# Inverse roots in columns of tokens, and six units of products kept back in the last chunk

## The reference

```python
x = x + 0.5 * swiglu_ffn(x, norm_ffn1, w_ffn1_in, w_ffn1_out)     # d_model 1024, d_ff 2816
h = rmsnorm(x, norm_mix) @ w_in                                    # columns for two head groups
y_ssd = rmsnorm(ssd(h) * silu(z), norm_ssd_out)                    # 512 wide
y_nsa = rmsnorm(sparse_attention(h), norm_nsa_out)                 # 512 wide, three branches
x = x + concatenate([y_ssd, y_nsa]) @ w_out
x = x + memory_attention(x, norm_mem_q, w_mem_q, w_mem_out)        # 4 heads, 256 memory rows
x = x + 0.5 * swiglu_ffn(x, norm_ffn2, w_ffn2_in, w_ffn2_out)
y = rmsnorm(x, norm_final)
rmsnorm(x, g) = x * rsqrt(mean(x * x) + 1e-6) * g
swiglu_ffn(x, g, w_in, w_out): gate, up = split(rmsnorm(x, g) @ w_in); return (silu(gate) * up) @ w_out
```

## Time and profile before

| | |
|---|---|
| median of three runs | 2847.9 us (2844.55 to 2849.76) |
| profiled execution | 2840.38 us |
| its span, first to last instruction | 2838.7 us |
| mean granted clock of TensorE | 0.973 of 2.4 GHz |
| TensorE busy (matmul) | 2697.9 us, 95% |
| VectorE busy | 1418.0 us, 50% |
| ScalarE busy | 717.4 us, 25% |
| GpSimd busy | 344.1 us, 12% |
| first feed-forward stage ends | near 817 us |
| output projection and queries | 1778.6 to near 1931 us |
| second feed-forward stage, final norm and stores | 2011 to 2838.7 us |

### The profile page before, as it was taken

One profiled execution on the slowest core, in us unless ns is written; L12 is line 12 of the kernel. 1 busy time (PEld: TensorE's weight loads), 2 busy tenths in 40 slices (PEclk: granted clock), 3 DMA queues, 4 the chain that ended last, 5 costly groups with the idle time before them and its releaser, 6 DMA issues. The chain is left out here.

```text
span 2838.7 us, 43914 instructions
## 1 busy us (share of the span) xinstructions
PE 2697.9 (95%) x17720; PEld 2529.8 (89%) x17720; DVE 1418.0 (50%) x2949; ACT 717.4 (25%) x1466; POOL 344.1 (12%) x294
## 2 busy tenths in 40 slices
PE   8999999999989998989789988899999999999996
PEld 7999999999989997879557765797899999999996
DVE  7444444444466222335567753676644444444445
ACT  5111111111042212212456652435411111111102
POOL 0000000000020000101157761220100000000003
PEclk9999999999999999989889998899999999999998
DMA  6111111111025325114120004102211111111101
GB/s 215 45 45 45 46 45 45 45 45 45 16 96 67 53 76 192 59 38 116 42 61 16 2 22 177 60 23 90 75 45 45 45 45 45 45 45 45 41 5 63
DMA packets 62989, 168.42 MB, mean 59 GB/s; under 512 B 10468, under 2 KB 43780, under 8 KB 52996
## 3 DMA queue, kind: packets, MB, share of 16 engines
q1 hardware_dynamic: 57716, 150.36, 16.8%
q10 hardware_dynamic: 3104, 9.41, 0.9%
q0 software_dynamic: 1968, 5.77, 0.6%
HBM read 145.90 MB, written 23.69 MB: 60 GB/s over the span
## 5 line engine op out<-in xcount | busy, mean ns | idle before, releaser
L523 DVE TENSOR_TENSOR ffn_gated<-ffn_gate_up,ffn_inv_rms 128x728 f32<-128x728 f32 x132 | 120.6, 914 | 536.9 <-PE ffn_gate_up L206 536.7
L204 PE MATMUL ffn_gate_up<-h_ffn_hi,ffn_up_hi 128*128 128x364 f32 (+1 forms) x1056 | 349.1, 331 | 15.1 <-DVE h_ffn_lo L102 11.5
L204 PE MATMUL ffn_down<-ffn_act_hi,ffn_down_hi 128*128 128x364 f32 (+1 forms) x1056 | 349.9, 331 | 7.8 <-issue 6.2
L204 PE MATMUL ffn_gate_up<-h_hi,ffn_up_hi 128*128 128x364 f32 (+1 forms) x1056 | 347.5, 329 | 2.6 <-DVE ffn_gated L523 1.0
L205 PE MATMUL ffn_gate_up<-h_ffn_lo,ffn_up_hi 128*128 128x364 f32 (+1 forms) x1056 | 347.8, 329 | 0.0
L205 PE MATMUL ffn_down<-ffn_act_lo,ffn_down_hi 128*128 128x364 f32 (+1 forms) x1056 | 347.8, 329 | 0.0
L206 PE MATMUL ffn_gate_up<-h_ffn_hi,ffn_up_lo 128*128 128x364 f32 (+1 forms) x1056 | 347.7, 329 | 0.0
L206 PE MATMUL ffn_down<-ffn_act_hi,ffn_down_lo 128*128 128x364 f32 (+1 forms) x1056 | 347.3, 329 | 0.0
L205 PE MATMUL ffn_gate_up<-h_lo,ffn_up_hi 128*128 128x364 f32 (+1 forms) x1056 | 346.9, 329 | 0.0
L206 PE MATMUL ffn_gate_up<-h_hi,ffn_up_lo 128*128 128x364 f32 (+1 forms) x1056 | 346.9, 328 | 0.0
L557 DVE SCALAR_TENSOR_TENSOR x<-ffn_down,x 128x364 f32<-128x364 f32 (+1 forms) x480 | 248.0, 533 | 148.0 <-PE ffn_down L206 148.0
(11 more groups left out here) (469 smaller groups left out, 4739.5 us busy)
## 6 DMA issues: line engine op xcount, KB each, us to landing
ffn_up_raw<-in_w_ffn_in SPq DMA_DIRECT2D x42, 1024.0 KB, 4.8
ffn_down_raw<-in_w_ffn_out SPq DMA_DIRECT2D x22, 1024.0 KB, 4.8
mix_w_raw<-in_w_mix SPq DMA_DIRECT2D x20, 512.0 KB, 3.4
scratch_x<-x SPq DMA_DIRECT2D x1, 4352.0 KB, 12.8
out_proj<-mix_stage ACTq DMA_DIRECT2D x8, 544.0 KB, 2.7
x<-scratch_x SPq DMA_DIRECT2D x1, 4352.0 KB, 16.9
cmp_w<-in_cmp_w SPq DMA_DIRECT2D x2, 2048.0 KB, 14.6
ssd_pages<-in_cmp_pages SPq DMA_DIRECT2D x32, 128.0 KB, 2.0
```

Of the source, the lines that this page charges most:

```text
L204: pe.matmul(out, w_hi, x_hi, start=start, stop=False)
L523: dve.tensor_tensor(zu[:, b, :, 0:w], gu[:, b, :, 0:w], inv[:, groups(g)].rearrange("p (o c) -> p o c", o=1).to_broadcast([P, 2, w]), ALU. ...
```

## The change

It has four parts.

1. **Last chunk of both feed-forward stages.** TensorE makes only tiles 0 to 5 of the down product before `up(c, 1)`, and tiles 6 and 7 (six units) after it. The high and low parts of the last down weights are made in two pieces (columns 0 to 767 at the old place, 768 to 1023 when the six units are through), so that the low-part semaphore counts one more; SP's load of the next stage's weights waits for it. The last f = 1 products go into the idle buffers of the gate/up weights, so that the parts still being read stay whole. ACT loads the root's table behind the last silu.
2. **Final norm.** The sum over partitions is made with the squares as stationary operand and one moving column, so that 128 tokens land in the 128 partitions of one column (three columns a group); root and reciprocal work on three columns; a second product with the column spread over the stationary operand and the identity moving brings the inverse roots into all partitions, in PSUM; the scale reads them there. The last group's last squares don't go over GpSimd. `lag` becomes 3, the sums stand behind closing unit 10 and 18, the spreadings behind 12 and 20. Stores of the last group take two tiles each.
3. **Head of the output projection.** The same form for the two norms of the first token group. One throwaway ahead of the sums, two behind the spreadings, instead of seven.
4. **Sample attention.** ACT loads the root's table at its end.

New functions (`BLOCKS` is 3), the final norm, and the constants; the size of a store stands in `stores`:

```diff
+def column_sums(pe, out, squares, mean, width, start, stop):
+    for j in range(BLOCKS):
+        mm = pe.matmul(out[:, j:j + 1], squares[:, block_at(j, width)], mean[:, 0:1], start=start and j == 0,
+                       stop=stop and j == BLOCKS - 1)
+def columns_to_all(pe, core, out, columns, width):
+    for j in range(BLOCKS):
+        mm = pe.matmul(out[:, block_at(j, width)], columns[:, j:j + 1].to_broadcast([P, P]), core.ident, start=True,
+                       stop=True)
...
 class FinalNorm:
+    def sum(self, pe, g, last, direct=None):
+        run, mean, w = self.running, self.core.mean_model, width_of(g)
+        pe.wait_ge(run.added, last + 1)
+        mm = column_sums(pe, self.at(self.sums, g), run.acc[g], mean, w, True, direct is None)
+        if direct is not None:
+            pe.wait_ge(run.sq_ready, direct + 1)
+            mm = column_sums(pe, self.at(self.sums, g), run.sq[direct % len(run.sq)], mean, w, False, True)
...
-        dve.reciprocal(self.inv[:, 0:width_of(g)], self.rms[:, 0:width_of(g)]).then_inc(self.inv_ready, 1)
+        dve.reciprocal(self.at(self.inv, g), self.at(self.roots_of, g)).then_inc(self.inv_ready, 1)
+    def to_all(self, pe, g):
+        pe.wait_ge(self.inv_ready, g + 1)
+        columns_to_all(pe, self.core, self.banks[:, g, :], self.at(self.inv, g), width_of(g)).then_inc(self.all_ready, 1)
     def scale(self, dve, g, k):
...
-                                 self.inv[:, 0:width_of(g)], ALU.mult, ALU.mult).then_inc(self.y_ready, 1)
+                                 self.banks[:, g, 0:width_of(g)], ALU.mult, ALU.mult).then_inc(self.y_ready, 1)
...
+            size = KT // 2 if g < GROUPS - 1 else 2
...
-        lag = 4
+        lag = 4 if final is None else 3
+        DEFERRED = (KT - 2) * GROUPS
+        deferred = slice(DEFERRED // GROUPS * P, D_MODEL)
...
-                    sp.wait_ge(down_lo_ready, chunks)
+                    sp.wait_ge(down_lo_ready, chunks + 1)
```

ACT in the last chunk:

```diff
+                        act.wait_ge(dn_ready, (c - 1) * (KT * GROUPS) + DEFERRED)
+                        act.activation(down_hi[:, :, 0:deferred.start], down_raw[:, :, 0:deferred.start], ACT.Copy
+                                       ).then_inc(down_hi_ready, 1)
                     gate(c, 1)
...
+                        act.activation(root_table[:], core.eps[:, 0:1], ACT.Sqrt)
+                        act.wait_ge(dn_ready, c * (KT * GROUPS))
+                        act.activation(down_hi[:, :, deferred], down_raw[:, :, deferred], ACT.Copy
+                                       ).then_inc(down_hi_ready, 1)
```

TensorE in a chunk and in the closing:

```diff
                 def chunk(c, par, more, full):
                     up(c, 0)
                     if full:
-                        down(c - 1, 1 - par)
+                        down(c - 1, 1 - par, 0, KT if more else KT - 2)
                     up(c, 1)
+                    if not more:
+                        down(c - 1, 1 - par, KT - 2, KT)
...
+                        if t == KT - 2:
+                            pe.wait_ge(down_lo_ready, c + 2)
...
+                        elif d in (KT - 1 + lag, 2 * KT - 1 + lag):
+                            fin.sum(pe, d // KT - 1, d - lag)
+                        elif d in (KT + 1 + lag, 2 * KT + 1 + lag):
+                            fin.to_all(pe, d // KT - 1)
```

DVE in a chunk and in the closing:

```diff
                     for g in range(GROUPS):
-                        multiply(c, 1, par, g)
+                        multiply(c, 1, par, g, more)
...
+                        add(c - 1, DEFERRED, KT * GROUPS)
+                        split_down(c + 2, deferred)
...
-                    ahead = KT + lag + 1
+                    ahead = KT + lag + 2
...
+                        if fin is not None and d in (KT + lag, 2 * KT + lag):
+                            fin.invert(dve, d // KT - 1)
```

Head of the output projection, ACT, then TensorE (`sum_first(k)` is now `column_sums` of one tile), then DVE. `first_root(0)` stands ahead of the eighth square:

```diff
-                root(0)
-                root(1)
                 w_hi(0)
+                first_root(1)
...
-                sum_first(0)
-                sum_first(1)
-                throwaway(pe, core, ps[:, R - 1, :], 7)
+                throwaway(pe, core, ps[:, R - 1, :], 1)
+                for k in range(KT - 2):
+                    sum_first(k)
+                first_to_all(0)
+                for k in range(KT - 2, KT):
+                    sum_first(k)
+                first_to_all(1)
+                throwaway(pe, core, ps[:, R - 1, :], 2)
...
-                invert(0)
-                pair_of("mixed", 0, 0)
+                first_invert(0)
+                normed_pair("mixed", 0, 0)
+                first_invert(1)
+                low_pair("mixed", 0, 0)
                 w_lo(0)
-                invert(1)
                 pair_of("mixed", 0, 1)
```

More of the change, by code:

```diff
@@ L165, with __init__ @@
 class FinalNorm:
[L168 removed]
+    def __init__(self, core, xT, gain, running, sums, banks, roots, inv, store):
         self.core, self.xT, self.gain, self.running, self.store = core, xT, gain, running, store
[L170 to L179 removed]
+        self.sums, self.banks, self.roots_of, self.inv = sums, banks, roots, inv
+        self.summed, self.rms_ready, self.inv_ready, self.all_ready, self.y_ready, self.stored = map(
+            core.sem, ("fin_summed", "fin_rms_ready", "fin_inv_ready", "fin_all_ready", "y_ready", "y_stored"))
@@ L181, in invert @@
+    def roots(self, act, g):
+        act.wait_ge(self.summed, g + 1)
+        act.activation(self.at(self.roots_of, g), self.at(self.sums, g), ACT.Sqrt, bias=self.core.eps[:, 0:1]
+                       ).then_inc(self.rms_ready, 1)
     def invert(self, dve, g):
         dve.wait_ge(self.rms_ready, g + 1)
[L183 to L186 removed]
+        dve.reciprocal(self.at(self.inv, g), self.at(self.roots_of, g)).then_inc(self.inv_ready, 1)
@@ L192, in stores @@
     def stores(self, sp):
-        half = KT // 2
+        n = 0
         for g in range(GROUPS):
-            for part in range(2):
-                sp.wait_ge(self.y_ready, g * KT + (part + 1) * half)
-                sp.dma_start(self.store[:, part * half:(part + 1) * half, groups(g)],
-                             self.xT[:, part * half:(part + 1) * half, groups(g)]).then_inc(self.stored, 16)
-        sp.wait_ge(self.stored, 16 * 2 * GROUPS)
+            size = KT // 2 if g < GROUPS - 1 else 2
+            for k in range(0, KT, size):
+                sp.wait_ge(self.y_ready, g * KT + k + size)
+                sp.dma_start(self.store[:, k:k + size, groups(g)], self.xT[:, k:k + size, groups(g)]
+                             ).then_inc(self.stored, 16)
+                n += 1
@@ L359, in close @@
                         running.square(act, d, xT[:, t, groups(g)])
-                        if fin is not None and d in (KT + lag, 2 * KT + lag):
+                        if fin is not None and d in (KT - 1 + lag, 2 * KT - 1 + lag):
                             fin.roots(act, d // KT - 1)
@@ L427, in _ @@
             def _(pool):
-                for d, (t, g) in enumerate(closing[:summed_here]):
+                for d, (t, g) in enumerate(closing[:added_here]):
                     running.add(pool, d, g, t == 0)
@@ L461, in up, with down @@
                             parts.late_sums(pe)
-                def down(c, par):
-                    pe.wait_ge(down_lo_ready, c + 1)
-                    pe.wait_ge(act_ready, c * 6 + 6)
-                    for t in range(KT):
+                def down(c, par, first=0, last=KT):
+                    if not first:
+                        pe.wait_ge(down_lo_ready, c + 1)
+                        pe.wait_ge(act_ready, c * 6 + 6)
+                    for t in range(first, last):
                         for g in range(GROUPS):
@@ L3005, in _, with sum_first, first_to_all @@
             def _(pe):
-                def sum_first(s):
-                    for k in range(4 * s, 4 * s + 4):
-                        pe.wait_ge(sq0_ready, k + 1)
-                        pe.matmul(ms[:, s, :TG], core.mean_inner[:], first_squares[k % 4], start=k == 4 * s,
-                                  stop=k == 4 * s + 3).then_inc(sq0_summed, 1)
+                def sum_first(k):
+                    pe.wait_ge(sq0_ready, k + 1)
+                    column_sums(pe, sums0[:, k // 4, :], first_squares[k % 4], core.mean_inner, TG, k % 4 == 0,
+                                k % 4 == 3).then_inc(sq0_summed, 1)
+                def first_to_all(n):
+                    pe.wait_ge(inv0_ready, n + 1)
+                    columns_to_all(pe, core, ms[:, n, :], inv0[:, n, :], TG).then_inc(all0_ready, 1)
                 def sum_of(i):
                     unit = UNITS[i]
-                    pe.wait_ge(rms_ready, i - 1)
+                    if i < 4:
+                        pe.wait_ge(h_ready["mixed", 0], 4 * (i - 1))
+                    else:
+                        pe.wait_ge(rms_ready, i - 3)
                     if unit[0] == "x":
```

143 lines of the change are left out of this document (91 added, 52 removed).

## The result

The changed kernel takes 2824.3 us (median of 4 runs, 2819.74 to 2824.88), the kernel before 2848.8 (4 runs, 2844.55 to 2851.18): ratio 0.9912, 95% interval 0.9895 to 0.9929, so between 20 and 30 us less. In a later group of runs it was 2822.8 against 2839.8, ratio 0.9939 (0.9916 to 0.9963). The forecast, 2825.5 and 22.4 us less, lies in both intervals, and faster was right. One of its terms was wrong all the same: the head of the output projection, forecast at 2.2 us, brings next to nothing. The other terms hold within half a us each in this trace; in five later ones the last norm takes 0.7 to 1.2 us more. That the median fell 1.2 us from the forecast is luck: by what was measured the terms add up to 20.0, and the two groups of runs say 24.5 and 17.0.

What follows compares the result with a forecast made beforehand. TensorE is busy 95% of the span, so gains lie only in its waits, low clock, or after its last product. 4.65 + 15.1 + 0.5 + 2.2 = 22.4 us off 2847.9 gives 2825.5; range 2819 to 2833.

Steps and rivals of the forecast that it cites:

- Six units, first stage: First feed-forward stage's closing: six kept down units cover TensorE's wait, 3.10 us, and avoid the slow clock, 1.55; together 4.65.
- Six units, last stage: Last feed-forward stage's closing: the same cover gains 3.10 us for the wait and 2.75 for the clock.
- The last norm: Last stage, first closing product to last scale: 46.9 us becomes 34.9, gain 12.0, including 2.75 of slow clock.
- Stores: Behind the last scale: the halved last store lands sooner, between nothing and 1.0 us; 0.5 taken.
- Head of the output projection: Start of the output projection: second product over at 1807.0 instead of 1809.27, gain 2.2 us, bounds -1.4 to 6.4.
- The step on the clock: Output projection's head: the column sums run at 1.2 GHz, at twice the full-clock prices, 1.3 us each.
- The row that the step leaned on: Products with 32 moving columns from 1769.8 on: TensorE worked without pause, yet the granted clock stayed at 0.50.
- Downstream TensorE is fed, so the head's gain is kept.: Output projection behind its head: TensorE never lacks work, so the 2.2 us gained there stay gained.
- Full clock in the head: Output projection's head: sums reach full clock as before; gain 26.6 us, total 2821.3. Chance 0.27.
- The wait only moves: Both feed-forward closings: a late add or second split holds them, clock falls; gain only 11.9 us, 2836.0. Chance 0.07.
- The low clock goes on behind the sums: First products behind the head's sums: each costs 3.3 us more; nine give +7.3, 2855. Chance 0.02.
- Little is left: Later stages: the clock falls elsewhere, gains largely offset, total within 0.2% of before. Chance 0.03.

Runs made afterwards that it cites:

- norm alone: The kernel before with only the new final norm and its stores; 2831.4 us, ratio 0.9968.
- head alone: The kernel before with only the new output-projection head and the root table loaded in the sample attention; 2842.4 us, ratio 1.0006.
- the first trace: First profiled execution of the changed kernel, all four parts, against the kernel before; 2824.16 us.
- the last kernel: Changed kernel with folded head squares, weights' high parts one product earlier behind the second group's squares, two direct final-norm squares; 2814.8 us, ratio 0.9896 against before.

## Why the prediction was right, point by point

*Six units, first stage.* Forecast 4.65. From gate/up's end to the fourth add, less the six units, it is 9.06 - 4.19 = 4.9. Right; the fourth add of the closing is 4.2 us behind its start, as taken. But only the 3.10 of the wait is a fixed gain: the 1.55 of the clock is that of one trace, and in the three traces with the old turns (before, norm alone, head alone) it is 1.6, 0 and 2.8.

*Six units, last stage.* Forecast 5.85 (3.10 and 2.75), measured 10.27 - 4.20 = 6.1. Right. Here the clock's part is 2.8, 1.5 and 2.8 in the same three. That the queues have room was right too, and three units would have been enough.

*The last norm.* Forecast 34.9 us from closing start to last scale, measured 35.4, and 36.1 to 36.6 in the five traces of this norm in which the clock falls before the last spreading. The prices held: six records of sums in 0.83 us with their tail, spreading the same, the last add over at 27.6 against 27.45, scales 0.52. The missing half us is the last group's chain: GpSimd's last add ends 28.3 us after the closing's start, not 28.0, and the reciprocal is over at 30.3, not 29.8. What the forecast didn't price is that these sums and the spreading can run at the lower clock too, for 0.7 to 1.2 us.

*Stores.* Forecast 0.5, measured nothing (4.14 and 4.08 us behind the last scale). The term's reason, a shorter last store, is void: with the scales close together the stores are in a queue. In the trace of the norm alone the DMA share is 0.99 or more from 2.7 us ahead of the last scale to 2.3 behind it. The 6.1 in the first trace is another matter, and told above.

*Head of the output projection.* The step on the clock came out right: the lower level through all column sums in every kernel that has them, 1.28 us a square where 1.3 was taken, and the last low part 23.3 us behind the first square where 23.7 was worked out. The clock then fell again in the trace of the changed kernel, at 1798.4 for 3.4 us, and the second product was over after 29.5 us instead of 28.3. The row that the step leaned on carries it less than the prediction had it: the same products of 32 columns that ran at 0.50 before ran at 1.00 in the changed kernel (1.12 us a row and not 1.92), so which level they had says more of where the clock had fallen than of the products. That column sums stay at the lower level is shown by the nine traces that have them in the head. But the step that failed is the last one: "Downstream TensorE is fed, so the head's gain is kept." It isn't. DVE and ACT pace the stage from their last low part on, 38.2 us to the second group, and by the forecast's own figures that low part didn't move. The head is worth 0, with 0.35 us at most; 2.2 were forecast. The trace of before had the sign: TensorE waits 0.32 us for DVE and 1.29 us for GpSimd there, 59 and 62 us behind the first square, so it was not fed throughout, and the prediction looked no further than the head.

*The sum.* By what was measured: 4.9 for the first stage, 50.11 - 35.44 = 14.7 for the last from gate/up's end to the last scale (less the six units), 0 for the stores, 0.35 for the head: 20.0 us, against 22.4. Two groups of runs say 24.5 and 17.0, so the total says little of any one term.

*Rivals.* Full clock in the head: out. The wait only moves: out. The low clock goes on behind the sums: it came for one short stretch in two of the nine traces, at 1798, far from the point where it decides. Little is left: not so, but its mechanism was seen at work, 3.8 us between the two traces in stages that nobody changed.

## What to carry to other kernels

A chain of small steps between two products is covered best by work of the product before that nobody waits for, and three units of a us each were enough where six were kept; with the wait goes the lower clock behind it, which in the trace of before was some two fifths of the gain at both turns (4.8 of 11.0 us), and in that of the norm alone 1.5 us at both together. A gain at a stage's head counts only if it moves the engine that paces the stage: measure it at the second group's first product, not at the head's own end. Where many stages run at a clock that falls at varying moments, compare stretches between the same two instructions, not totals.

## What the runs showed of the hardware that I had not expected

At the lower clock a sum over partitions costs no less in columns than wide: three matmuls of one moving column take 1.28 us, one of 364 columns 1.21. At the upper one three take 0.67 to 0.69 (2809.26 to 2809.95), and a wide one 0.61 (two records 0.306 apart, before, from 1783.85 on). In the one trace with an instruction packet 2.8 us ahead of the last scale, in the middle of the last stores, the kernel ended 2 us later than its scales would have it. And the total of a kernel moves by several us with the moments at which the granted clock falls: the twelve runs of the kernel with the head alone spread over 17 us, the six of the last kernel over 20.
